# Convolution, retention gate and delta gate projections of a hybrid decoder layer: ten pairs of seven half-size products instead of twenty full tiles, with a weight ring of two

## What is computed

```python
u = rmsnorm(h, norm_mix)
proj = jnp.einsum('bld,de->ble', u, w_in)
rq, rk, rv, rg, dqkv, dz, da, db, gate_a, gate_b = jnp.split(proj, _split_points(), axis=-1)
# widths: 256, 256, 512, rg 512, dqkv 1536, dz 512, 4, 4, 1024, 1024
...
o_r = rms_plain(o_r) * jax.nn.silu(rg)              # retention, then its swish gate
branch_a = o_r @ w_ret_up
xpad = jnp.concatenate([s_conv, dqkv], axis=1)      # causal depthwise convolution, width 4
conv = xpad[:, 0:L] * conv_w[0]
for j in range(1, CONV_W):
    conv = conv + xpad[:, j:j + L] * conv_w[j]
conv = jax.nn.silu(conv)
cq, ck, cv = jnp.split(conv, [DN_QK, 2 * DN_QK], axis=-1)
...                                                 # gated delta rule on cq, ck, cv
o_d = rms_plain(o_d) * dn_norm * jax.nn.silu(dz)
branch_b = o_d @ w_dn_up
merged = sigmoid(gate_a) * branch_a + sigmoid(gate_b) * branch_b
h = h + merged @ w_out
...                                                 # router, 16 experts, embedding gate, final norm
```

## Time and profile before

| | us |
|---|---|
| median of 3 runs | 820.5 |
| fastest, slowest of them | 820.47, 2129.68 |
| profiled execution, its own time | 822.27 |
| its span, first to last instruction | 820.4 |
| TensorE busy | 800.8 |
| VectorE busy | 403.3 |
| ScalarE busy | 221.5 |
| GpSimd busy | 153.9 |

### The profile page before, as it was taken

One profiled execution on the slowest core, in us unless ns is written; L12 is line 12 of the kernel. 1 busy time (PEld: TensorE's weight loads), 2 busy tenths in 40 slices (PEclk: granted clock), 3 DMA queues, 4 the chain that ended last, 5 costly groups with the idle time before them and its releaser, 6 DMA issues. The chain is left out here.

```text
span 820.4 us, 12782 instructions
## 1 busy us (share of the span) xinstructions
PE 800.8 (98%) x5136; PEld 501.3 (61%) x5136; DVE 403.3 (49%) x848; ACT 221.5 (27%) x483; POOL 153.9 (19%) x182
## 2 busy tenths in 40 slices
PE   9999999999999999999999999999899999999995
PEld 4445777778879987777777776455443333334443
DVE  4223456677656523664853458726352101104976
ACT  3211151595224311121101110122121111125275
POOL 0234321032055224200220044000100001004100
PEclk9999999999999999999999999999999999999998
DMA  9520364423020200524242123135899999995211
GB/s 358 214 102 1 110 207 155 141 92 111 1 104 3 93 13 13 206 66 109 103 191 69 48 103 131 53 132 195 310 404 354 424 424 421 407 395 194 76 52 64
DMA packets 21303, 136.40 MB, mean 166 GB/s; under 512 B 2492, under 2 KB 3276, under 8 KB 13948
## 3 DMA queue, kind: packets, MB, share of 16 engines
q1 hardware_dynamic: 13328, 103.08, 32.4%
q0 software_dynamic: 4720, 23.83, 7.9%
q10 hardware_dynamic: 3196, 8.66, 3.3%
HBM read 120.12 MB, written 19.64 MB: 170 GB/s over the span
## 5 line engine op out<-in xcount | busy, mean ns | idle before, releaser
L818 PE MATMUL pair<-mem 128*128 128x288 f32 x640 | 158.4, 407 | 0.0
L818 PEld LDWEIGHTS pair<-mem 128*128 128x128 f32 x640 | 120.5, 190 | 35.7 <-ACT mem L1504 1.6
L986 PE MATMUL single<-mem 128*128 128x288 f32 x448 | 110.0, 407 | 0.2
L986 PEld LDWEIGHTS single<-mem 128*128 128x128 f32 x448 | 84.7, 190 | 25.7 <-issue 1.6
L1371 PE MATMUL single<-mem 128*32 128x512 f32 x768 | 85.1, 594 | 0.9 <-DVE mem L2542 0.9
L1504 ACT ACTIVATE mem<-single 128x256 f32<-128x256 f32 (+6 forms) x104 | 41.9, 413 | 126.6 <-PE single L1232 48.5
L1504 ACT ACTIVATE mem<-pair 128x512 f32<-128x512 f32 (+5 forms) x83 | 36.6, 488 | 143.3 <-PE pair L1319 46.7
L2535 DVE SCALAR_TENSOR_TENSOR mem<-single,mem 128x256 f32<-128x256 f32 x12 | 5.8, 484 | 102.3 <-PE single L1371 91.1
L1371 PEld LDWEIGHTS single<-mem 128*32 128x32 f32 x768 | 23.6, 110 | 52.8 <-issue 51.7
L1223 PE MATMUL pair<-mem 128*128 128x512 f32 x112 | 51.0, 601 | 0.0
L1440 PE MATMUL pair<-mem 128*128 128x512 f32 x112 | 49.4, 595 | 0.3 <-DVE mem L2603 0.3
(11 more groups left out here) (433 smaller groups left out, 1126.2 us busy)
## 6 DMA issues: line engine op xcount, KB each, us to landing
mem<-in_w_gu SPq DMA_DIRECT2D x17, 2048.0 KB, 14.3
mem<-in_w_down SPq DMA_DIRECT2D x17, 1024.0 KB, 13.5
y_slots<-mem SPq DMA_DIRECT2D x9, 512.0 KB, 10.8
y_slots<-in_zeros POOLq DMA_DIRECT2D x8, 512.0 KB, 8.6
mem<-in_w_ga SPq DMA_DIRECT2D x2, 2048.0 KB, 8.5
mem<-in_w_gb SPq DMA_DIRECT2D x2, 2048.0 KB, 8.1
mem<-in_w_wo SPq DMA_DIRECT2D x2, 2048.0 KB, 8.1
mem<-in_w_pg SPq DMA_DIRECT2D x2, 2048.0 KB, 17.1
```

The source lines that it names most:

```text
L818: last = nc.tensor.matmul(pb[:, hf, 0:HALF], w(k), rhs[:, k, hf * HALF:(hf + 1) * HALF], start=(k == 0), stop=(k == kk - 1))
L986: last = nc.tensor.matmul(single[plan.buf[s]][:, 0:HALF], lhs[:, k, :], rhs[:, k, :], start=(k == 0 and j in (0, 1, 3, 4)), stop=(k == 3), ...
```

## The change

The twelve cv tiles, four rg tiles and four dz tiles become ten groups of two tiles: groups 0 to 5 are cv, 6 and 7 rg, 8 and 9 dz. A group is seven products of 4 matmuls of 128x288, over half of the input channels and half of the tokens, instead of 32 matmuls. Steps ("fa", g, name) are evacuated by ACT (p1, p5, p6, p4), steps ("fd", g, name) by DVE (p2, p3, p7). p6, p7 and p4 go on adding in the bank of p1, and p3 in that of p5, so each of them waits for the evacuation before it. The combinations of a group's weights are four POOL operations of 128x512 (step fS, two and two), the last of them in place. The combinations of the inputs (uS on DVE, usum) are made once, before group 0, and the merge gates use them too.

Silu of rg and dz is a step of its own (sw). The convolution buffer has four tiles, and the taps run over 600 contiguous columns. The ring has two places; the third holds usum and serves the last chunk. The order of the list is written anew; rg 2 and 3, which stood behind l1, are now group 7, whose products but the last stand ahead of l1.

```diff
-RING = 3
+def place(n):
+    return 2 if n == len(CHUNKS) - 1 else n % 2
...
+    def middle(g, p2=(), p5=(), p6=(), p3=()):
+
+        return ([f(g, "p2")] + list(p2) + [f(g, "p5")] + list(p5) + [f(g, "p6")] + silu(g - 1) + list(p6) + [("fS", g + 1, 0), f(g, "p3")]
+                + [("fS", g + 1, 1)] + list(p3) + [f(g, "p7")])
+
+    gather = [[("gK", t), ("gQ", t)] for t in range(NT)]
+    s += [("uS", 0), ("uS", 1), ("ab",), ("uS", 2), ("uS", 3), f(0, "p1"), ("abT",)]
...
+    s += [f(1, "p1"), ("rO4",)] + middle(1, p2=[("rUs", 0, 0), ("rUs", 0, 1)], p5=[("rUs", 1, 0), ("rUs", 1, 1)], p6=[("gC",), ("gG",)], p3=[("rOt",)] + nq)
+    s += taps(2) + [f(2, "p1"), f(1, "p4")] + taps(3)
+    s += middle(2, p2=[("gL",)], p6=[("gE", 0)]) + taps(4) + [("rN",), f(2, "p4")] + taps(5)
+    s += [f(3, "p1")] + middle(3, p2=[("nr", "rN")], p6=[("ns", "rN"), ("gE", 1), ("gE", 2)]) + taps(6)
+    s += [f(4, "p1"), f(3, "p4")] + taps(7) + middle(4, p2=[("nl", "rN")], p6=[("gE", 3), ("gE", 4)], p3=nf[0:2]) + taps(8)
+    s += [f(5, "p1"), f(4, "p4")] + taps(9) + middle(5, p2=[("gs", 0), ("gs", 1)] + nf[2:4], p5=[("gs", 2)], p6=[("gs", 3), ("gs", 4)], p3=[("gX",), ("gr",)])
+    s += taps(10) + [f(6, "p1"), f(5, "p4")] + taps(11)
+    s += middle(6, p5=sum(gather, []), p3=[("sw", 6, 0)]) + [("rgs", 0), f(7, "p1"), f(6, "p4"), ("sw", 6, 1), ("rgs", 1)]
+    s += [("gA", t) for t in range(NT)]
+    s += middle(7, p3=[("sw", 7, 0)])
     s += [("l1", t) for t in range(NT)]
-    s += [("rg", 2), ("rgs", 2), ("rg", 3), ("rgs", 3)]
     for v in LEVELS:
         on = [t for t in range(NT) if v in levels(t)]
-        s += [("lA", v, t) for t in on if v < 64] + [("lY", v, t) for t in on]
+        s += [("lA", v, t) for t in on if v < 64] + [("lY", v, t) for t in on[0:2]]
+        s += {2: [f(7, "p4"), ("rgs", 2), ("sw", 7, 1)], 4: [("rgs", 3)]}.get(v, []) + [("lY", v, t) for t in on[2:]]
...
+    s += [("sO", 0), ("sU", 0)] + dz(8, "p1") + dz(8, "p2") + [("sD", 1)] + dz(8, "p5") + [("sDs",)] + dz(8, "p6") + [("fS", 9, 0), ("sO", 1), ("sU", 1)]
+    s += dz(8, "p3") + [("fS", 9, 1), ("sO4",)] + dz(8, "p7") + [("sD", 2), ("sw", 8, 0)] + dz(8, "p4") + [("sO", 2), ("sU", 2)] + dz(9, "p1") + dz(9, "p2")
+    s += [("sw", 8, 1), ("sD", 3), ("sOt",)] + dz(9, "p5") + [("sUs", 0), ("sO", 3), ("sU", 3)] + dz(9, "p6") + [("sUs", 1)] + dz(9, "p3")
+    s += [("wS", 0, 0), ("wS", 0, 1), ("sUs", 2)] + dz(9, "p7") + [("sw", 9, 0), ("sUs", 3)] + dz(9, "p4") + [("sw", 9, 1)]
...
-                if n >= RING:
-                    mm_wait(sp, plan.chunk_last[n - RING])
+                if n >= 2:
+                    mm_wait(sp, ("wy", NFAST - 1, 6) if place(n) == 2 else plan.chunk_last[n - 2])
...
+                    if name in ("p5", "p6", "p3", "p7"):
+                        pe.wait_ge(sem("fsum"), 4 * g + {"p5": 1, "p6": 2, "p3": 3, "p7": 4}[name])
+                    for k in range(4):
+                        last = nc.tensor.matmul(group_bank(s), lhs[:, k, :], rhs[:, k, :], start=(k == 0 and name in ("p1", "p2", "p5")),
+                                                stop=(k == 3), skip_group_check=True)
...
+                    for j in range(1, CW):
+                        last = V.scalar_tensor_tensor(out=to, in0=cbuf[m % 4][:, j:j + 600], scalar=conv_w[:, m, j:j + 1],
+                                                      in1=to, op0=ALU.mult, op1=ALU.add)
...
+                elif k0 == "fS":
+                    if i == 0:
+                        pool.wait_ge(sem(f"ring{place(n)}"), landed(n))
+                        if g:
+                            mm_wait(pool, ("fa", g - 1, "p6"))
+                        G.tensor_tensor(wfast[0], w[1][0], w[1][1], ALU.add).then_inc(sem("fsum"), 1)
+                        pool.wait_ge(sem("fsum"), 4 * g + 1)
+                        G.tensor_tensor(wfast[1], wfast[0], w[0][0], ALU.subtract).then_inc(sem("fsum"), 1)
+                    else:
+                        if g:
+                            mm_wait(pool, ("fd", g - 1, "p3"))
+                        G.tensor_tensor(wfast[2], w[0][1], wfast[1], ALU.subtract).then_inc(sem("fsum"), 1)
+                        G.tensor_tensor(w[1][0], w[0][0], w[1][0], ALU.subtract).then_inc(sem("fsum"), 1)
```

More of the change, by code:

```diff
@@ L162, in const_layout, with landed @@
     return at, off
+def place(n):
+    return 2 if n == len(CHUNKS) - 1 else n % 2
+def landed(n):
+    return 16 if place(n) == 2 else 16 * ((n + 1) // 2)
 CHUNKS = ["qk", "v", "dq", "dk", "dv", "rg", "dz", "ga0", "ga1", "upr", "gb0", "gb1", "upd", "wo0", "wo1"]
 def schedule():
-    s = [("tk", k) for k in range(6)] + [("ss",), ("tk", 6), ("xr",)] + [("tmq", t) for t in range(NT)]
+    s = [("tk", k) for k in range(6)] + [("ss",), ("tk", 6), ("xr",)] + [("tmq", t) for t in range(4)]
+    s += [("fS", 0, 0), ("fS", 0, 1), ("tmq", 4)]
     for t in range(NT):
@@ L185, in schedule @@
[L185 to L193, removed]
+    f = lambda g, name: (("fd" if name in ("p2", "p3", "p7") else "fa"), g, name)
@@ L303, in own_banks @@
     if s[0] == "tmq":
-        return [("pair", s[1] // 2)] if s[1] < 4 else [("single", 0)]
+        return [("half", s[1])] if s[1] < 4 else [("single", 0)]
     return [("single", 1), ("single", 2)] if s[0] == "ss" else [("single", 3)]
@@ L314, in __init__ @@
         self.order, self.mm, self.buf, self.before, self.chunk_last = {}, {}, {}, {}, {}
-        count, nmm, npair, nsingle, last, half = {}, 0, 0, 1, {}, {}
+        count, nmm, nsingle, last, held = {}, 0, 1, {}, {}
+        age = lambda b: self.mm.get(last.get(("half", b)), 0)
         for s in self.steps:
@@ L348, in __init__ @@
                 self.mm[s] = nmm
[L349 to L350 removed]
+                self.buf[s], self.before[s] = s[2], [("uy", 1, 1, 1, (2, 5)[s[2]])]
+                last[("half", 2 * s[2])] = s
             elif k != "wo" and (k in PAIR or k in SINGLE):
@@ L353, in __init__ @@
                 self.mm[s] = nmm
-                key = ("pair", npair % 2) if k in PAIR else ("single", nsingle % 4)
-                if k in PAIR: npair += 1
-                else: nsingle += 1
-                self.buf[s] = key[1]
-                self.before[s] = last.get(key)
-                last[key] = s
+                if k in PAIR:
+                    i = 1 if k == "sUs" else min(range(2), key=lambda i: max(age(2 * i), age(2 * i + 1)))
+                    keys = [("half", 2 * i), ("half", 2 * i + 1)]
+                else:
+                    i = nsingle % 4
+                    keys = [("single", i)]
+                    nsingle += 1
+                self.buf[s] = i
+                self.before[s] = [last.get(key) for key in keys]
+                last.update({key: s for key in keys})
             if k in CHUNK_OF:
@@ L801, in bank_free @@
             def bank_free(s):
-                prev = plan.before[s]
-                if prev is not None and prev[0] != "warm":
-                    ev_wait(pe, prev)
+                for prev in plan.before[s]:
+                    if prev is not None and prev[0] != "warm":
+                        ev_wait(pe, prev)
             def chunk(s):
@@ L809, in chunk @@
                 if n:
-                    pe.wait_ge(sem(f"ring{n % RING}"), 16 * (n // RING + (n % RING > 0)))
-                return ring[n % RING]
-            def gemm_channels(s, w, rhs, kk, fresh=True):
-                pb = pair[plan.buf[s]]
-                for k in range(kk):
-                    for hf in range(2):
-                        last = nc.tensor.matmul(pb[:, hf, 0:HALF], w(k), rhs[:, k, hf * HALF:(hf + 1) * HALF],
-                                                start=(k == 0), stop=(k == kk - 1))
-                last.then_inc(s_mm, 1)
+                    pe.wait_ge(sem(f"ring{place(n)}"), landed(n))
+                return ring[place(n)]
             pe.wait_ge(sem("rtmp_ones"), 1)
```

293 lines of the change are left out of this document (172 added, 121 removed).

## The result

The changed kernel takes 844.7 us (median of 4 runs, 843.5 to 845.9), the kernel before 820.5 us on the same chip: a ratio of 1.029, 95% interval 1.0274 to 1.0307. The 820.5 us are the median of three executions; a fourth took 2129.68 us and is not counted. The forecast of 825.3 us was wrong, and so was its range of 810 to 836.

A forecast was written before the change was run, and what follows sets the result against it. The prediction took TensorE, busy 98% of the span, as the bound. Savings of 20.9 and 0.9 us against added waits and slow clock came to +4.8 on 820.4, or 825.2; it forecast 825.3 us, range 810 to 836.

The forecast's parts named there:

- What the products save: Twenty full tiles on TensorE become ten groups of seven products at 1.964 us each: 20.9 us less.
- The clock: TensorE's clock halves in the idle time ahead of the levels, so p4(7) takes double: 2.0 us more.
- stays low through the levels: Rival: the clock stays at 1.2 GHz through the levels, 12 us in place of 2.0, 835 us; chance 0.10.
- l1 loses its cover: Ahead of the first lY, TensorE idles while l1's chain runs behind group 7: 11.5 us more (10.5 to 12.5).
- rN behind gE(0): Group 2: ACT evacuates rN behind two Silus and gE(0), so TensorE waits ahead of p1(3): 3.0 us (1.3 to 5).
- fS(4) behind gE(1), gE(2): Group 3: on POOL these stand ahead of fS(4)'s first sum, so TensorE waits for p5(4): 3.8 us (2.5 to 5).
- fS(5): Group 4: the first weight sum comes at 11.7 against 10.8, behind gE(4), so TensorE waits 0.9 us (0 to 3).
- abT: Softplus and sigmoid of abT, with two table loads, stand ahead of the copy of p5(0): 0.6 us.
- gr: Group 5: DVE waits in gr for gs 4 and a root, ahead of p7(5)'s addition: 0.5 us (0 to 2).
- The sUs steps: State steps: sUs(1) waits 1.2 us for POOL, sUs(3) 2.7 for DVE's sums; together 3.9 us (2 to 6).
- The weight loads: Loading weights into a ring of two places is covered by the products between and costs nothing.
- POOL starves DVE: Rival: POOL holds up DVE's tap blocks, TensorE waits for banks in groups 1 to 5, 3 us each: 840 us; chance 0.09.

The follow-up runs named there:

- after: The changed kernel itself, with no follow-up edit; 844.7 us, ratio 1.029 to the kernel before.
- e7: Changed kernel with l1 ahead of group 7's products, group 8's weight sums at level 16, gr and gE later, wS behind sUs(3); 823.2 us.
- b1: The kernel before with one move, rg 2 and 3 ahead of the l1 steps; ratio 1.0145 to the kernel before.
- e1: Changed kernel with the five l1 steps moved right behind gA, ahead of the products of group 7; 837.9 us.
- e6: As e1, with group 8's four weight sums also moved to the mask of level 16; ratio 1.0107 to the kernel before.
- e2: Changed kernel with GpSimd's 40 weight sums cut to 16 of 512 columns, so output and routing differ; 859.7 us, only the stage is read.
- e5: Changed kernel with the gE steps moved behind the weight sums and the root they stood ahead of; 840.7 us.
- c2: Changed kernel with wS(0,0) and (0,1) moved between sUs(0) and sU(3); 837.1 us.
- e9: As e7, but with wS(0,0) and (0,1) between sUs(0) and sU(3); 819.7 us, ratio 0.9989 to the kernel before.
- e4: Changed kernel with 12 matmuls of 128x512, whose result nobody reads, in the gap ahead of the first lY; 847.8 us.
- e8: As e9, with the second two of each group's four weight sums on VectorE instead of GpSimd; 815.7 us, ratio 0.9942 to the kernel before.

## Why the prediction was wrong, step by step

- **What the products save** (20.9): it was 8.9 in TensorE's busy time, 12.0 less. Two things are in that. The larger is the clock (next point). The other is the price: the 65 products of after that ran wholly at 2.4 GHz take 2.01 us in the mean, from their start to that of the next step, not 1.964. In a row of five they take 1.94 (9.86 for 40 records); many stand alone between other kinds of work and take 2.04 to 2.14. e7 has the same products and only one stretch at 1.2 GHz, 140.9 to 144.3, of which 3.3 us are busy: its 232.2 us are 15.5 less than before, and would be about 17 without that stretch. So about 4 us of the 20.9 never were to be had. That the neighbours make the price is read from timelines and was not tried by itself.
- **The clock** (2.0, put behind one gap): the step failed, though that gap was priced about right. Behind l1's wait p4(7) took 2.81 us for 1.96 and the first 32 records of lY 1.97 for 1.28 (e7), 1.5 us together. But the clock also fell behind three other waits, which had no term: p4(5) and the next two products took 7.89 us for 5.9, the two behind the 3.73 us wait for fS(4) took 2.81 and 3.21 for 1.96 each, and p4(9) behind the 4.8 us at sUs(3) took 3.59 for 2.2. In all, 15.1 us of TensorE's busy time in the stage lie in windows of granted clock 0.50 (167.4 to 170.8, 198.1 to 204.9, 242.5 to 256.1, 351.7 to 358.5); half of it, 7.5 us, is the estimate of what they cost. The rival "stays low through the levels" did not come: in after the rate is back 3 us after the first lY.
- **l1 loses its cover** (11.5, 10.5 to 12.5): right in mechanism, 13.1 us, and b1, e1 and e6 show it. Two things make the 1.6 us more. The end of the first mask was read as a quarter of a merged row, 231.9, but in the kernel before this mask alone takes 1.48 us from 231.13, beside a product of VectorE (the others take 0.63): the chain was 11.6 us there already, not 10.9. And the last sum of fS(8), 240.14 to 241.40, runs beside l1's first two products on VectorE, which take 1.81 us instead of 0.85. I had counted fS(8) for GpSimd's load and not for its place; in e2, with short sums, the wait is 12.1.
- **rN behind gE(0)** (3.0): 2.7, and e5 takes it away, so the order was the cause. The reason given for its size was half of it: the held-up taps and the load of g_rows end together in after, and e2, without the hold-up, waits 3.9. That the number fits is partly luck. **fS(4) behind gE(1), gE(2)** (3.8): 3.7, right, and e5 takes it away. **fS(5)** (0.9, ahead of p5(5)): none in after, 1.7 and 1.9 in e1 and e6. What after has nearby, 0.9 ahead of p3(4) for ScalarE's evacuation of p5(4), no term had. abT (0.6): 1.0.
- **gr** (0.5, 0 to 2): 5.5 us, the largest miss of one term. I took gs 4 to be ready by the order of the list. The two blocks of taps ahead of it took 7.5 and 9.4 us, 3.5 alone, beside a GpSimd without rest, in a stretch where I had counted GpSimd's load (5.1 us a group) but not that gE(3), gE(4), fS(5) and fS(6) follow each other.
- **The sUs steps** (3.9): 6.1 us, 1.3 at sUs(1) (forecast 1.2) and 4.8 at sUs(3) (2.7, of which the hold-up beside GpSimd was 1.3). c2 shows that wS beside GpSimd's three instructions is the whole of the 4.8.
- **The weight loads** (0): right; no product waits for a weight. The loads of g_rows and n_rows, which the forecast does not mention, do reach TensorE by way of ScalarE and VectorE (e2, e5, e7, e9).
- **POOL starves DVE** (rival, 0.09, 840 us): it came true in part. I had the hold-up in two terms, rN and sUs, and none in the others. The doubled tap of the earlier trace rows was in view; its use should have been a price for all of VectorE's work beside 54.7 us more of GpSimd in the stage. e2, which takes 42.7 of them away, says 21.5 us of VectorE's time; of the stage it is 3 to 9 us, and 4.6 more for wS (c2), which is held up by GpSimd's old work.

What held: the change has no gain as it is ordered, and idle time added is more than load saved. What failed is the price of the saving (20.9, of which low clock and lone products took 12.0), the waits on a VectorE held up by GpSimd (ahead of p4(5) and sUs(3), 10.3 us for 3.2), and 1.6 us of l1's chain.

## What to carry to other kernels

When work is taken off the bounding engine, list for every chain of the other engines which piece of it was the cover, and put that chain's start ahead of the piece that remains: one move of the five l1 steps was worth 7 us here, and two moves together took away 12. Price a second engine's added work not by its own load alone but also by how much longer the other engine's instructions take beside it, and look where its instructions follow without a gap. Do not place an instruction that others wait for behind one that itself waits; check that before moving work to another engine, since the same move cost 24 us in one order and gained 4 in the other. Look at one instruction by itself before taking a share of a merged row. And before an edit is given a gain, compare two traces in a stretch that it does not touch: here such a stretch differed by 5 us.

## What the hardware showed

- **VectorE beside GpSimd in a row.** A VectorE instruction beside GpSimd's can take twice its time (three taps 5.28 us for 2.60), but it can also stand through a whole row: the sum at 346.06 above, 4.28 us beside three instead of 0.68, and a tensor-scalar instruction of 128x600 in after, 4.89 us beside four, 0.53 alone. The Trainium skill, page "SBUF — State Buffer", section "Who interferes with whom", says that a VectorE instruction with two SBUF inputs contends with a GpSimd instruction that reads SBUF, that a tensor-scalar instruction can contend too, and of the latter kind that the one issued first holds the shared ports for the whole instruction while the other blocks. That they contend, the trace agrees. Here a VectorE instruction stood through three and four GpSimd instructions in a row.
- **The clock falls soon and returns late.** The granted clock was 0.50 after 2.8 us of idle TensorE in e4 and after 3.73 us in after (0.85 in 166 to 168, 0.50 in 168 to 170), but stayed 1.00 from 140 to 148 in after, across 2.74 us of idle time. It came back 3 to 6 us after work did. The Trainium skill, page "TensorE: Matmul & The Clock Gate", Part 1, says that only sustained work brings the full rate back; the windows agree.
- **Scatter of the first 35 us.** The kernel before and b1 have the same code up to here, yet the first cv starts at 84.66 and at 81.97. The longest record of the first projections (L857) is 1222 ns in one and 697 in the other, where 592 is the median; the granted clock reads 1.00 in both from 5 to 15, so this record of it does not explain the doubling. Up to 2.7 us of difference there mean nothing, after's 1.8 neither.
- **Left open.** The reordered kernels scatter more (e7 817.8 to 827.0 in 10 runs, e8 813.6 to 821.1 in 12) than the kernel before (819.3 to 823.8 in 23). No run here tells why, nor why one and the same order takes up to 5 us less or more from the stage's start to p7(7)'s end.
